# Hybrid decoder step on one core: attention units in another order, convolution moved out of the attention stage, prompt mask loaded in the stage before

## What is computed

```
h = rms_norm(x)                         # 544 x 1024
[q | k | v | glu] = h @ w_in            # 12 heads of 64, 256 convolution channels
q, k = rope(q), rope(k)
attn = merged dilated causal windows    # (128,1), (512,4), (2048,16), one softmax over the union,
                                        # a key that n windows reach counts n times
conv = swish(layer_norm(depthwise_conv31(g) + b))
x += concat(attn, conv) @ w_out
x += peer(rms_norm(x))                  # 8 heads, 128x128 product keys, top 16, two expert tables
y = rms_norm(x)
```

## Time and profile before

| | |
|---|---|
| median of 3 runs | 2163.32 us (2163.17 to 2169.2) |
| the profiled execution, its own time | 2165.74 us |
| its span in the trace | 2163.9 us |
| TensorE busy | 2004.1 us (93%), 9593 matmul records |
| VectorE busy | 1454.9 us (67%) |
| ScalarE busy | 678.4 us (31%) |
| GpSimd busy | 398.4 us (18%) |
| mean granted TensorE clock | 0.922 of full |
| `project` | 0 to 217 us of the span |
| `mix` | 217 to 490 us |
| `route` with the out projection first | from 490 us on |

### The profile page before, as it was taken

One profiled execution on the slowest core, in us unless ns is written; L12 is line 12 of the kernel. 1 busy time (PEld: TensorE's weight loads), 2 busy tenths in 40 slices (PEclk: granted clock), 3 DMA queues, 4 the chain that ended last, 5 costly groups with the idle time before them and its releaser, 6 DMA issues. The chain is left out here.

```text
span 2163.9 us, 27907 instructions
## 1 busy us (share of the span) xinstructions
PE 2004.1 (93%) x9593; PEld 1706.4 (79%) x9593; DVE 1454.9 (67%) x3120; ACT 678.4 (31%) x1032; POOL 398.4 (18%) x473
## 2 busy tenths in 40 slices
PE   7999699999999996998699999999999999998884
PEld 6885466784577663776599999999999999997783
DVE  1113863211299996999778787888888887876554
ACT  2221232201111111989333333333333333323222
POOL 0000000000023322000232443443333323310000
PEclk9999555759999998999899999999999999999997
DMA  8000500212222111454688887898988888864433
GB/s 324 18 15 20 199 0 1 103 44 93 101 69 78 59 46 62 154 205 175 251 287 282 290 300 259 299 314 275 322 289 298 293 283 292 289 202 129 122 111 112
DMA packets 195788, 382.10 MB, mean 177 GB/s; under 512 B 13167, under 2 KB 134957, under 8 KB 192269
## 3 DMA queue, kind: packets, MB, share of 16 engines
q1 hardware_dynamic: 157733, 243.52, 33.3%
q0 software_dynamic: 36864, 134.23, 17.5%
q10 hardware_dynamic: 1056, 2.62, 0.3%
HBM read 343.51 MB, written 35.34 MB: 175 GB/s over the span
## 5 line engine op out<-in xcount | busy, mean ns | idle before, releaser
L1204 PE MATMUL bank<-p_high,v_high 128*128 128x416 f32 x1024 | 363.2, 355 | 29.3 <-DVE v_low L1608 29.1
L1204 PE MATMUL bank<-p_high,v_low 128*128 128x416 f32 x1024 | 361.8, 353 | 0.0
L1204 PE MATMUL bank<-p_low,v_high 128*128 128x416 f32 x1024 | 358.4, 350 | 0.0
L1158 PE MATMUL bank<-h_high,u_high 128*128 128x416 f32 x768 | 273.1, 356 | 23.2 <-DVE u_low L1608 19.1
L1158 PE MATMUL bank<-h_high,u_low 128*128 128x416 f32 x768 | 273.6, 356 | 0.0
L1158 PE MATMUL bank<-h_low,u_high 128*128 128x416 f32 x768 | 270.9, 353 | 0.0
L1374 POOL DMA_INDIRECT rows<-in_u_rows,row_u x128 | 173.7, 1357 | 472.3 <-issue 246.1
L1204 PEld LDWEIGHTS bank<-p_high,v_high 128*128 128x128 f32 x1024 | 192.7, 188 | 42.2 <-DVE v_low L1608 40.8
L1608 DVE TENSOR_TENSOR v_low<-vv,v_high 128x1024 fp32r<-128x1024 f32 x128 | 156.8, 1225 | 101.8 <-ACT v_high L1301 93.9
L1307 ACT CAST p_high<-gel 128x416 fp32r<-128x416 f32 x128 | 69.1, 540 | 460.1 <-DVE gel L1636 457.5
L413 PE MATMUL proj<-w_in_sb,xT 128*128 128x256 f32 (+1 forms) x880 | 193.8, 382 | 14.2 <-DMA w_in_sb<-in_w_in 14.2
(11 more groups left out here) (203 smaller groups left out, 2932.1 us busy)
## 6 DMA issues: line engine op xcount, KB each, us to landing
vv<-in_v SPq DMA_DIRECT2D x128, 512.0 KB
u<-in_uT SPq DMA_DIRECT2D x96, 512.0 KB
gates_kept<-staged SPq DMA_DIRECT2D x13, 2048.0 KB, 7.5
gate<-gates_kept SPq DMA_DIRECT2D x30, 832.0 KB
early<-in_uT SPq DMA_DIRECT2D x32, 512.0 KB, 3.6
w_in_sb<-in_w_in SPq DMA_DIRECT2D x4, 2048.0 KB, 21.6
wq<-in_w_q SPq DMA_DIRECT2D x16, 512.0 KB, 3.5
ckT<-in_ckT SPq DMA_DIRECT2D x8, 768.0 KB, 5.8
```

What stands on the lines that cost most here:

```text
L1158: ins = pe.matmul(a_ps[par][:, 0:DT], x[:, par, k], y, start=(k == 0 and n == 0), stop=(k == KT - 1 and n == 2))
L1204: ins = pe.matmul(y_ps[m % 4][:, 0:DT], x[:, of % 2, c, at:at + P], y, start=(c == 0 and n == 0), stop=(c == CG - 1 and n == 2))
```

## The change

- `units` now has tile 3 first, then tile 2, then tiles 1 and 0 with one sample behind every three units. The samples' step numbers are 27, 31, ... 55.
- The convolution of the prompt's tiles 0 to 2 is done by VectorE in `project`, behind `take(i)`: 62 instructions of 128 columns for each tile. That of tile 3 is done by GpSimd in `mix`, as a multiply and an add for each tap and half (`tap` under `gpsimd`). VectorE keeps the samples' taps in `mix`, two instructions in each of the steps 0 to 30.
- The prompt mask is loaded in `project` into the place of the token rows, when their squares are taken. The convolution weights are loaded in `project` too.
- q is scaled by -1/8 when it is copied into `qT`, the masks change sign, the row maximum becomes a minimum, and the instruction that made the negated maximum (L682) is gone; ScalarE waits for `maxed` itself.
- The turns through `c_ps` are one sorted list (`turns`): heads of tile 3 at steps 16 and 17, of tile 2 at 28 and 29, convolution at 34 to 36, of tile 1 at 43 and 44, gated values at 49 to 51, of tile 0 at 59 and 60, behind the last unit. `norm_y` is at steps 37 to 42.
- The load of `w_out` is issued behind those of the third sample.

```diff
-    return np.where(count > 0, np.log(np.maximum(count, 1)) / SCALE, NEG).astype(np.float32)
+    return np.where(count > 0, -np.log(np.maximum(count, 1)), -NEG).astype(np.float32)
...
+        at = -(-nc.sbuf_base // 32) * 32
+        xtok = sb("xtok", [P, 2, D])
+        pmask = s["pmask"] = nc.alloc_sbuf_tensor_at("pmask", [P, 4, SEQ], F32, offset=at)
+        s["wo_at"] = at - KT * D * 4
...
+            sp.dma_start(cw[:], d.conv_w).then_inc(conv_in, 16)
+            sp.dma_start(cb[:], d.conv_b).then_inc(conv_in, 16)
             sp.dma_start(d.out_cs[:, 0:TAPS - 1 - DEC_T], d.state_rows[:, DEC_T:TAPS - 1]).then_inc(kept_stored, 16)
             for i in range(TILES):
                 r = ROWS[i]
+                if i == 3:
+                    sp.wait_ge(squared, TILES)
+                    sp.dma_start(pmask[:], d.pmask).then_inc(s.pmask_in, 16)
...
                         for j in range(4):
                             m = 4 * b + j
-                            dst = (qT if m < PAIRS else kT)[:, m % PAIRS, cols(i)]
-                            ins = nc.vector.tensor_copy(dst, src[:, j])
+                            if m < PAIRS:
+                                ins = nc.vector.tensor_scalar(qT[:, m, cols(i)], src[:, j], -SCALE, None, ALU.mult)
+                            else:
+                                ins = nc.vector.tensor_copy(kT[:, m - PAIRS, cols(i)], src[:, j])
...
+            def taps(i):
+                dve.wait_ge(turn_read, 4 * (i + 1))
+                if i == 0:
+                    dve.wait_ge(conv_in, 32)
+                for k in range(TAPS):
+                    for c in range(2):
+                        before = 2 * (TAPS * i + k - 1) + c + 1
+                        x, acc, w = gp[:, c, i * P + k:(i + 1) * P + k], y[:, c, cols(i)], cw[:, c, k:k + 1]
+                        if k == 0:
+                            nc.vector.tensor_scalar(acc, x, w, cb[:, c:c + 1], ALU.mult, ALU.add).then_inc(tapped, 1)
+                        else:
+                            dve.wait_ge(tapped, before)
+                            nc.vector.scalar_tensor_tensor(out=acc, in0=x, scalar=w, in1=acc, op0=ALU.mult,
+                                                           op1=ALU.add).then_inc(tapped, 1)
             for i in range(TILES):
                 rope(i)
                 if i + 2 < TILES:
                     mean(i + 2)
                     invert(i + 2)
                 take(i)
+                if i < LATE_TAPS:
+                    taps(i)
...
-    units = [(i, h) for i in range(4) for h in range(NH)] + [(4, b) for b in range(DEC_B)]
+    units = [(i, h) for i in (3, 2) for h in range(NH)]
+    short = [(i, h) for i in (1, 0) for h in range(NH)]
+    for b in range(DEC_B):
+        units += short[3 * b:3 * b + 3] + [(4, b)]
     U = len(units)
-    UP = 4 * NH
-    CATS = [NH * (i + 1) + 4 + n for i in range(4) for n in range(2)]
-    Y_TURNS = [43, 44, 45]
-    CAT_BEFORE_Y = sum(t < Y_TURNS[0] for t in CATS)
-    NORM_AT = 46
-    BACK = [54, 55, 56]
+    assert U == 4 * NH + DEC_B
+    of_sample = [units.index((4, b)) for b in range(DEC_B)]
+    turns = [(units.index((i, NH - 1)) + 5 + b, "heads", (i, b)) for i in range(4) for b in range(2)]
+    turns += [(34 + n, "conv", (n,)) for n in range(3)] + [(49 + n, "gated", (n,)) for n in range(3)]
+    turns.sort(key=lambda x: x[0])
+    NORM_AT = 37
     RING, V_RING = 3, 4
+    def turn_number(what, *args):
+        return [x[1:] for x in turns].index((what, args))
...
-            sp.dma_start(pmask[:], d.pmask).then_inc(mask_in, 16)
             sp.dma_start(smask[:], d.smask).then_inc(mask_in, 16)
-            sp.dma_start(cw[:], d.conv_w).then_inc(conv_in, 16)
-            sp.dma_start(cb[:], d.conv_b).then_inc(conv_in, 16)
             sp.dma_start(lng[:], spread(d.ln_g, [P, CH])).then_inc(ln_in, 16)
             sp.dma_start(lnb[:], spread(d.ln_b, [P, CH])).then_inc(ln_in, 16)
-            sp.dma_start(s.wo[:], d.w_out).then_inc(s.wo_in, 16)
             for b in range(DEC_B):
                 if b >= RING:
-                    sp.wait_ge(scored, UP + b - RING + 1)
+                    sp.wait_ge(scored, of_sample[b - RING] + 1)
                 sp.dma_start(ckT[:, b % RING], d.ckT[b]).then_inc(ck_in[b % RING], 16)
                 if b >= V_RING:
-                    sp.wait_ge(summed, UP + b - V_RING + 1)
+                    sp.wait_ge(summed, of_sample[b - V_RING] + 1)
                 sp.dma_start(cv[:, b % V_RING], d.cv[b]).then_inc(cv_in[b % V_RING], 16)
+                if b == 2:
+                    sp.dma_start(s.wo[:], d.w_out).then_inc(s.wo_in, 16)
...
+            def tap(k):
+                for c in range(2):
+                    x, w = gp[:, c, LATE_TAPS * P + k:SEQ + k], cw[:, c, k:k + 1]
+                    acc = y[:, c, LATE_TAPS * P:SEQ]
+                    if k == 0:
+                        nc.gpsimd.tensor_scalar(acc, x, w, cb[:, c:c + 1], ALU.mult, ALU.add).then_inc(tapped, 1)
+                    else:
+                        wait(pool, tapped, 2 * (k - 1) + c + 1)
+                        nc.gpsimd.tensor_scalar(term[:, c], x, w, None, ALU.mult).then_inc(term_ready, 1)
+                for c in range(2 if k else 0):
+                    pool.wait_ge(term_ready, 2 * (k - 1) + c + 1)
+                    acc = y[:, c, LATE_TAPS * P:SEQ]
+                    nc.gpsimd.tensor_tensor(acc, acc, term[:, c], ALU.add).then_inc(tapped, 1)
+            pool.wait_ge(qbd_ready, 2 * PAIRS)
+            for k in range(TAPS):
+                tap(k)
...
-                act.wait_ge(neg_ready, u + 1)
+                act.wait_ge(maxed, u + 1)
                 if u >= 3:
                     act.wait_ge(turned, u - 2)
-                nc.scalar.activation(pr[0:r, u % 3, 0:n], sm[0:r, u % 3, 0:n], ACT.Exp, bias=nmx[0:r, u:u + 1],
-                                     scale=SCALE, accum_out=den[0:r, u:u + 1]).then_inc(exped, 1)
+                nc.scalar.activation(pr[0:r, u % 3, 0:n], sm[0:r, u % 3, 0:n], ACT.Exp, bias=mx[0:r, u:u + 1],
+                                     scale=-1.0, accum_out=den[0:r, u:u + 1]).then_inc(exped, 1)
...
                 if u == 0:
-                    dve.wait_ge(mask_in, 32)
+                    dve.wait_ge(pmask_in, 16)
+                if u == of_sample[0]:
+                    dve.wait_ge(mask_in, 16)
                 if u >= 3:
                     dve.wait_ge(exped, u - 2)
-                mask = pmask[:, i, 0:n] if u < UP else smask[:, h]
+                mask = pmask[:, i, 0:n] if not sample(u) else smask[:, h]
                 nc.vector.tensor_tensor_reduce(out=sm[0:r, u % 3, 0:n], in0=s_ps[u % 3][0:r, 0:n], in1=mask,
-                                               scale=1.0, scalar=-3.0e38, op0=ALU.add, op1=ALU.max,
+                                               scale=1.0, scalar=3.0e38, op0=ALU.add, op1=ALU.min,
                                                accum_out=mx[0:r, u:u + 1]).then_inc(maxed, 1)
-                dve.wait_ge(maxed, u + 1)
-                nc.vector.tensor_scalar(nmx[0:r, u:u + 1], mx[0:r, u:u + 1], -SCALE, None,
-                                        ALU.mult).then_inc(neg_ready, 1)
...
-                    if h == 0 and i >= 2:
-                        dve.wait_ge(cat_turned, 2 * (i - 1))
+                    if h == 0 and i < 2:
+                        dve.wait_ge(c_turned, turn_number("heads", i + 2, 1) + 1)
...
+            def tap(k):
+                for c in range(2):
+                    x, w = gs[:, c, :, k:k + DEC_T], cw[:, c, k:k + 1]
+                    acc = y[:, c, SEQ:T].rearrange("p (b t) -> p b t", t=DEC_T)
+                    if k == 0:
+                        nc.vector.tensor_scalar(acc, x, w, cb[:, c:c + 1], ALU.mult, ALU.add).then_inc(sample_tapped, 1)
+                    else:
+                        dve.wait_ge(sample_tapped, 2 * (k - 1) + c + 1)
+                        nc.vector.scalar_tensor_tensor(out=acc, in0=x, scalar=w, in1=acc, op0=ALU.mult, op1=ALU.add
+                                                       ).then_inc(sample_tapped, 1)
...
-            dve.wait_ge(conv_in, 32)
-            for t in range(U + 4):
+            for t in range(U + 6):
                 if t < U:
                     row_max(t)
                 if 0 <= t - 1 < U:
@@ -793,14 +824,13 @@
                     tap(t)
                 if 0 <= t - 4 < U:
                     norm(t - 4)
-                if t in CATS:
-                    take_cat(CATS.index(t) // 2, CATS.index(t) % 2)
-                if t in Y_TURNS:
-                    take_y(Y_TURNS.index(t))
+                for n, (at, what, args) in enumerate(turns):
+                    if at == t:
+                        dve.wait_ge(c_turned, n + 1)
+                        by = {"heads": take_heads, "conv": take_conv, "gated": take_gated}[what]
+                        by(*args).then_inc(c_taken, 1)
                 if NORM_AT <= t < NORM_AT + 6:
                     norm_y(t - NORM_AT)
```

(52 more changed lines are left out.)

100 lines of the change are left out of this document (31 added, 69 removed).

## The result

The changed kernel takes **2135.14 us** (median of 4 runs, 2131.44 to 2136.97); the kernel before took 2166.26 us on the same chip (4 runs, 2163.17 to 2172.78). The ratio is **0.984**, 95% interval 0.981 to 0.988: 1.6% faster, clear of no change. The forecast was 2142 us.

What follows compares the result with a forecast made beforehand. TensorE was taken to bound the kernel, at half clock through most of `mix`. Terms -8.4 - 7.3 + 0 + 3.5 - 9 = -21.2 us took 2163.3 to 2142 us; 8-in-10 range 2088 to 2158 us.

Steps and rivals of the forecast that it cites:

- The start: Start of `mix`: early mask and convolution weights remove TensorE's idle wait before the first row minimum, -8.4 us.
- Taps in `project`: VectorE in `project`: 62 taps a tile at 0.26 us, 16 us within 18.9 us of slack, cost 0.
- VectorE bounds `project`: Rival in `project`: taps above 0.305 us each make TensorE stand still between tiles; 2178 us at 0.5 us; chance 0.06.
- Prompt taps out of tile 0's steps: Tile 0 in `mix`: units then cost what TensorE needs, -7.3 us, bounds -5 to -9 us.
- GpSimd: GpSimd in `mix`: 124 tap instructions, some 0.4 us each, together 50 us, done before step 34, cost 0.
- The order's end and the exposed waits: `mix`: tile 0's heads turned behind the last sample, +1.5 us; last sample's and ScalarE's exposed work, +2 us.
- The clock: Samples in `mix`: 5.8 us of full clock for each of eight, 46 us instead of 34, -9 us.
- 240 us at half clock: `mix` before the change: the stage is TensorE's at half clock for 240 us, only some 17 us belonging to others.
- long tiles at full clock: Rival in `mix`: tiles 3 and 2 run at full clock, tile 1 gains too, -70 us, 2093 us; chance 0.23.

Runs made afterwards that it cites:

- the doubled taps: The changed kernel with every tap of tiles 0 to 2 in `project` done twice, 124 instructions a tile instead of 62: 2188.6 us, ratio 1.009.
- the run with two products: The changed kernel plus two extra 512-column matmuls, results unused, behind the last transposes of `project`: 2095.6 us, ratio 0.967.
- the old order with products: The changed kernel with units in the earlier order (short rows first, samples last) plus two unused dense matmuls ending `project`: 2147.55 us, ratio 0.992.
- the burst at the start of `mix`: The changed kernel plus six extra unused matmuls as the first work of `mix`: median 2140.84 us.

## Why the prediction was right

*The start* (-8.4 us): TensorE's idle time in 217.2 to 226.8 us went from 8.41 to 0.67 us, -7.7. Loading the mask late by itself costs 5.2 us. The first row minimum waited for TensorE alone.

*Taps in `project`* (0): VectorE's and then ScalarE's timeline around the change of tiles of the earlier trace rows:

```profile
126.58 15.84 DVE L407 SCALAR_TENSOR_TENSOR catT_then_yT<-gp,cw,catT_then_yT 128x128 f32<-128x128 f32 x60
...
144.08 1.75 DVE L363 TENSOR_TENSOR qkr<-qk,cos 128x1536 f32<-128x1536 f32 x1
```

```profile
145.94 1.20 ACT L311 ACTIVATE qk<-proj,rstd 128x256 f32<-128x256 f32 x3 [9.48 <-DVE qkr L363]
```

60 taps in 15.84 us are 0.264 us each; 0.26 was said. The cosine product ends at 145.83 instead of 128.8 us, about 2 us inside the limit that the earlier trace rows gave (148.2 less ScalarE's copy; 137.8 and three times 3.4 us make 148.0). ScalarE waited 9.5 us for it and TensorE not at all. The rival "VectorE bounds `project`" fell on its own number, and the doubled taps show that its mechanism was real.

*Prompt taps out of tile 0's steps* (-7.3): with the start's term it made 15.7 us, and the old order alone gave 16.1 in the trace and 21.9 by the medians. In the new order long units stand where the taps were, and what the taps would cost there depends on where they lie: in steps 0 to 30 `mix` is 8.2 us longer (medians 11.1), in steps 0 to 15 7.2 (9.8). So the size came out right, but "tile 0's steps" describes the old order only.

*GpSimd* (50 us, hidden): the groups by shape say more, still hidden, since the last tap ends near 285 us and the first turn of the convolution (step 34) is at 352 us:

```profile
L571 POOL TENSOR_SCALAR term<-gp,cw 128x128 f32<-128x128 f32 x60 | 36.1, 614 | 0.0
L575 POOL TENSOR_TENSOR catT_then_yT<-catT_then_yT,term 128x128 f32<-128x128 f32 x60 | 26.1, 456 | 0.0
```

The two-input one, 0.46 us, is near what its neighbours in the earlier trace rows promised; the one-input one, which no row of before showed, takes 0.61 us where 0.4 was taken: 62 us together, inside the bounds of 35 and 78.

*The order's end and the exposed waits* (+1.5 and +2): the turns of tile 0's heads stand alone at the end, as forecast, with the out projection behind them:

```profile
455.49 1.11 PE L640 MATMUL c_ps<-ident,attn 128*128 128x128 f32 x4
457.38 0.69 PE L640 MATMUL c_ps<-ident,attn 128*128 128x128 f32 x2 [0.78 <-DVE catT_then_yT L769]
458.86 2.90 PE L1120 MATMUL bank<-wo,catT_then_yT 128*128 128x512 f32 x3 [0.78 <-PEq L490]
```

TensorE idles twice for 0.78 us here; before, it idled once for 0.73. Between the first sample's score and the out projection it idles for 4.9 us in all (318.8 to 459.0 us), where the samples' part had 0.4: 4.5 us more, against 3.5 forecast.

*The clock* (-9) was **the term that was mis-sized**: full clock for 59 us in place of 34, not 46; at 0.75 us each that is -19. The step that was short is "I take 5.8 us for each, between 3.4 us and some 8 us": the mean is 7.2 us, and the first three samples, with the longer units behind them, got 7.0 to 10.2. TensorE's busy time in `mix` says the same without a price for a microsecond: 256.75 us before and 236.10 after for the same work, -20.7. The run with samples last has 31.7 us of full clock and 17.8 us more of `mix`; (59 - 31.7) x 0.75 = 20.5 would be the clock's part, against which stand the waits between short units. With 59 us of full clock the sum is -7.7 - 7.3 + 3.5 - 19 = -30.5 us; the profiled executions differ by 28.8 and the medians by 31.1. The forecast of -21.2 fell 10 us short of the measured -31.1, and the clock's term accounts for that.

Two readings in the forecast were slips and change nothing: a `weigh` at half clock takes 1.73 us from start to start in the earlier trace rows (375.76 to 377.49), not 1.63, and of the "240 us at half clock" the samples' part has 34 us at full clock, as the forecast itself counts further on.

*The rival "long tiles at full clock"* was right in its price, 2093 us, and failed in its condition alone. The prediction held against it that 131 us of these units, without a gap, stayed at 0.50. That is true and says only that they don't raise the clock. Whether they keep it no row of before showed; in the run with two products they keep it for all 24 long units. The Trainium skill's rule ("TensorE: Matmul & The Clock Gate", "Why this matters for your kernels"), that a TensorE kept busy gets the full clock, is half borne out: with the hand-over filled the long rows kept it to their end, while TensorE at work for 26.70 of 26.70 us in the old order with products stayed at 0.50.

What stays open: what exactly makes the clock fall. The changed kernel loses it inside an unbroken run of scores, after a gap of 2.22 us; a gap of 1.17 us behind a dense product did no harm. Whether a shorter gap without a product would do, and whether the late mask or the taps in steps 0 to 30 would also spoil the effect of the products, was not run.

## What to carry to other kernels

Ask of each stretch at half clock two questions, not one: does this work raise the clock, and would it keep the clock if it were handed it? The second is worth a look at the few microseconds ahead of the stretch: here one dead product of 1.1 us was worth 40 us, more than the whole change. But here it only worked with long work directly behind it (long rows first) and no other engine in TensorE's way there (taps elsewhere): two edits worth 12 and 10 us at half clock (the order, the taps; first column of the table) were each worth some 50 with the clock held (second column), so edits should be tried in pairs before one is thrown away.

## What the runs showed of the hardware

*VectorE beside GpSimd.* The same two taps of 32 columns, three times while GpSimd does its own taps and once after it is done:

```profile
224.41 1.21 POOL L571 TENSOR_SCALAR term<-gp,cw 128x128 f32<-128x128 f32 x2
...
224.75 0.40 DVE L764 SCALAR_TENSOR_TENSOR catT_then_yT<-gs,cw,catT_then_yT 128x32 f32<-128x32 f32 x2
...
229.40 0.68 DVE L764 SCALAR_TENSOR_TENSOR catT_then_yT<-gs,cw,catT_then_yT 128x32 f32<-128x32 f32 x2
...
233.56 0.88 POOL L575 TENSOR_TENSOR catT_then_yT<-catT_then_yT,term 128x128 f32<-128x128 f32 x2
...
234.04 0.78 DVE L764 SCALAR_TENSOR_TENSOR catT_then_yT<-gs,cw,catT_then_yT 128x32 f32<-128x32 f32 x2
...
294.06 0.40 DVE L764 SCALAR_TENSOR_TENSOR catT_then_yT<-gs,cw,catT_then_yT 128x32 f32<-128x32 f32 x2
```

A pair takes 0.40 us alone. Of the 14 pairs that ran while GpSimd did taps (224 to 285 us) nine took 0.51 to 1.53 us, and each of the nine ran for 0.27 us or more beside GpSimd's two-input addition. Of the other five, at 0.39 to 0.42 us, three lay wholly beside its one-input multiplication, as the first above, and two met only the last 0.2 us of an addition. The Trainium skill has the rule ("SBUF — State Buffer", "Who interferes with whom"): a VectorE instruction with two inputs in SBUF contends with a GpSimd instruction that reads SBUF. The trace agrees for the two-input addition; beside the one-input multiplication, which reads SBUF as well, it shows none (in the run with two products one such pair took 0.59 us). In the changed kernel the contention costs nothing that shows, since VectorE has room under long units.

*Scores back to back overlap more than whole products do.* In the runs with one and two products, at full clock, one product over all 128 rows takes 1.12 us and two take 1.98. One score of 512 keys takes 1.12 us too, but three back to back take 1.95. Their heads lie in rows 0 to 63 and 64 to 127 in turn; that this is the reason is likely, but no run has them in the same half.

*The same kernel can have two times.* With the burst at the start of `mix` one program took 2092 us once and 2141 to 2147 us three times, with mean granted clocks of 0.961 and 0.935 to 0.937: where a short wait decides over the clock of a long stretch, one run can't tell the time.
